# The second layer's filler products on TensorE given up at its three norms

## Chip, cores and metric

The kernel runs on one core of a Trainium2 chip. The metric is the device time in microseconds of one execution; the time before is the median of three.

## Reference

Two transformer blocks one after the other, float32, on 256 tokens of width 1024. The first block and the first layer of the second block (a state-space and attention mixer) are untouched but for the last thing that TensorE does in the mixer. What matters here is the end of that layer and the whole of the last one:

```python
x = x + g1 * mix                                     # end of the hybrid mixer (layer 0)
h = rms_norm(x, norm_ffn_g[0]) * (1 + sc2) + sh2     # norm A
x = x + g2 * swiglu(h, w_gate[0], w_up[0], w_down[0])
h = rms_norm(x, norm_mix_g[1]) * (1 + sc1) + sh1     # layer 1
u = a * sigmoid(gt)            # a, gt = split(h @ w1 + b1)
u = causal_depthwise_conv(u, w_dw, b_dw)             # 31 taps
u = silu(layer_norm(u, ln_g, ln_b))                  # norm B
x = x + g1 * (u @ w2 + b2)
h = rms_norm(x, norm_ffn_g[1]) * (1 + sc2) + sh2     # norm C
x = x + g2 * swiglu(h, w_gate[1], w_up[1], w_down[1])
return rms_norm(x, final_norm_g)
```

`swiglu(h, wg, wu, wd)` is `(silu(h @ wg) * (h @ wu)) @ wd`, hidden width 2816. The document calls the three norms at which the change acts A, B and C.

## The kernel before

Each engine has its own program, written out by hand; semaphores order them. The program is made of blocks (`with nc.Block()`), and at the end of a block all engines meet before any goes on. The mixer of layer 0 is one block, whose end is recorded under line 1790; all that follows, norm A included, is the next.

**Tiling.** The tokens are two halves of 128 (`TT` = 2); the width is 8 pieces of 128 (`KT` = 8). A product of float32 operands is two instructions on TensorE, a transpose is one. Weights stream through a ring of 1 MB slots, filled by SyncE's queue and given back by TensorE (`used`).

**The fillers.** `keep_clock(pe, bank, n)` (line 141) issues n products of the identity with itself, 128x256 out, into a PSUM bank that is free at that place. Nothing waits for them and nobody reads their output. It is called in six places; three of them are touched.

**Norm A.** The mixer's output products (line 2027, `out_half`) end in four parts; VectorE combines each into `X` (lines 2225 and 2227), ScalarE sums the squares (2152). TensorE's last entry in the block is a wait for VectorE's reads (`read_a`) and `keep_clock(pe, 3, 6)`. In the next block VectorE adds up the sums (3138, 3037), ScalarE takes the root (2949), VectorE inverts it and scales the two halves of `X` into `xn` (3046). TensorE turns each half with eight transposes (2698, `turn`), VectorE and ScalarE move the turned pieces with scale and shift into `HT` (3052, 2954), and `first_rows` (2711) starts the first gate product piece by piece as `HT` appears. Then the chunks of the feed-forward part: `half_rows` (2718), the seven-product scheme `seven` (`product`, 2747; `down_part`, 2724; `turn_hid`, 2757), `last_down` (2733).

**Layer 1 up to norm B.** One more norm, with other products of TensorE in its gap (2852, 2858), then the pointwise product, the convolution (part on TensorE, 2873, part on VectorE), the means (2862), `gate_rows` (2858), and the variance (2922). Then `keep_clock(pe, 5, 6)`. ScalarE takes the root (3009), VectorE inverts it (3225) and multiplies (3228), and ScalarE applies silu in eight pieces (3013). The second pointwise product (2932) takes its first eight products one by one as those pieces appear; it has 64 products in all.

**Norm C.** After the last of them `keep_clock(pe, 7, 5)`. VectorE gates and adds the last quarter (3237, 3241), ScalarE sums squares (3020), then as at A: 3243, 3244, 2949, 3042, 3046, the transposes of `turn(2)`, and `ffn(1, 2)`.

Of the kernel before, what the change touches and what calls it, by code (L numbers as in the profile page):

```python
# [66 lines left out]
def _program(nc, t, out, top):  # L67
# [26 lines left out]
    def clear_retired(pool, old):  # L94
        for _, s in old:
            pool.sem_clear(s)
# [9 lines left out]
    def bc(ap, axis, n):  # L106

        v = ap.unsqueeze(axis)
        shape = list(v.shape)
        shape[axis] = n  # L110
        return v.broadcast_to(shape)
# [29 lines left out]
    def keep_clock(pe, bank, n):  # L141

        for _ in range(n):
            pe.matmul(PS[:, bank, 0:S], ident[:], bc(ident[:], 1, 2), start=True, stop=True)
# [153 lines left out]
    with ExitStack() as scope:  # L298
# [60 lines left out]
        def stage_a(k):  # L359
# [19 lines left out]
        FINISH = [("g", 0, 31), ("g", 1, 40), ("r", 0, 48), ("g", 2, 51), ("r", 1, 54), ("g", 3, 57), ("r", 2, 60),  # L379
                  ("g", 4, 67)]  # L380
        square_at = {at: f for f, (_, _, at) in enumerate(FINISH)}
        mean_at = {at + 1: f for f, (_, _, at) in enumerate(FINISH)}
        scale_at = {at + 2: f for f, (_, _, at) in enumerate(FINISH)}
        finish_of = {(kind, j): f for f, (kind, j, _) in enumerate(FINISH)}
# [1226 lines left out]
    with ExitStack() as scope:  # L1611
# [178 lines left out]
        with nc.Block() as block:  # L1790
# [16 lines left out]
            def _(pe):  # L1807
# [237 lines left out]
                pe.wait_ge(read_b, 1)  # L2045
                out_half(1, 1)
                pe.wait_ge(read_a, 2)
                keep_clock(pe, 3, 6)

            @block.scalar  # L2050
            def _(act):
# [602 lines left out]
    with nc.Block() as block:  # L2654
# [38 lines left out]
        def _(pe):  # L2693
            def turn(n):
                for i in range(TT):
                    pe.wait_ge(scaled, TT * n + i + 1)
                    for k in range(KT):
                        mm = pe.transpose(turned_bank(k)[:, i * P:(i + 1) * P],  # L2698
                                          xn[:, i, :].rearrange("p (m k) -> p k m", k=KT)[:, k, :], ident[:])
                        if i == TT - 1:  # L2700
                            mm.then_inc(turned, 1)
# [219 lines left out]
                for m in range(2 * quarter, 2 * quarter + 2):  # L2921
                    mm = pe.matmul(PS[:, 7, 0:S], meanw[:], SQ[:, m, :], start=(m == 0), stop=(m == KT - 1))  # L2922
            mm.then_inc(made, 1)
            keep_clock(pe, 5, 6)
            for c in range(4):
                arrive(pe, B_PW2 + c)
                w = w_slot(B_PW2 + c)
# [4 lines left out]
                        mm = pe.matmul(PS[:, 2 + c, i * CW:(i + 1) * CW], SQ[:, k, i * P:(i + 1) * P], w[:, k, :],  # L2932
                                       start=(k == 0), stop=(k == KT - 1))
                mm.then_inc(used, 1)
            keep_clock(pe, 7, 5)
            turn(2)
            ffn(1, 2)

# [437 lines left out]
```

## Time and profile before

| | |
|---|---|
| time, median of 3 runs | 1472.97 us (1471.86, 1472.97, 1478.15) |
| time of the profiled execution | 1474.04 us |
| its span | 1472.3 us |
| mean granted TensorE clock | 0.981 of full |
| busy: PE, DVE, ACT, POOL | 1382.5, 811.6, 248.1, 259.0 us |

The span runs from the first to the last instruction of the profiled execution, and positions such as "at 903" are microseconds from its start; 1.74 us of that execution's time lie outside its span. PE is TensorE's product instructions, PEld its weight loads, DVE VectorE, ACT ScalarE, POOL GpSimd. The granted clock is given as a share of full speed (2.4 GHz); its other level is half of that.

### The profile page before, as it was taken

The page shows a single profiled execution, that of the slowest core. Times are in us where ns is not written, and L with a number is a line of the kernel's source. Part 1 is how long each engine was busy: PE and PEld are TensorE (multiplying, and loading weights), DVE is VectorE, ACT ScalarE, POOL GpSimd, SP SyncE. Part 2 cuts the span into 40 slices and gives each one's busy share as a digit, 9 for nine tenths or more (in the row PEclk, how much of TensorE's full clock was granted, in tenths as well). Part 3 has the DMA queues.
Part 4 walks back from the last instruction along what each step waited for, and adds up shares of the span by engine and source line. Part 5 has one row for each costly group of instructions (what it writes and reads, how often), then busy time and mean ns, then how long its engine had stood idle before and what let it go on. Part 6 is the DMA issues. An engine that isn't in the chain of part 4 may idle for free. (4 is left out here: it accounts for less than half of the span.)

```text
span 1472.3 us, 18919 instructions
## 1 busy us (share of the span) xinstructions
PE 1382.5 (94%) x7561; PEld 1018.4 (69%) x7561; DVE 811.6 (55%) x1405; ACT 248.1 (17%) x530; POOL 259.0 (18%) x342
## 2 busy tenths in 40 slices
PE   5999999988757999999999999999999999999997
PEld 1877655644333888778888888777776868777774
DVE  2458785332223677853544674888744963544432
ACT  2221211000001211322435101000002032000001
POOL 5078010000001100543436304000021000000000
PEclk9999999998888999999999999999999999999999
DMA  9976788899999588846773456988853633545530
GB/s 345 324 253 230 273 341 328 366 415 416 417 418 369 184 299 290 298 142 157 182 174 117 143 171 201 333 323 326 311 183 103 215 94 115 168 151 168 166 120 29
DMA packets 176055, 355.57 MB, mean 242 GB/s; under 512 B 7289, under 2 KB 137040, under 8 KB 158560
## 3 DMA queue, kind: packets, MB, share of 16 engines
q1 hardware_dynamic: 166720, 313.64, 59.8%
q0 software_dynamic: 9248, 40.71, 9.5%
q8 instruction: 61, 1.00, 0.3%
q14 instruction: 26, 0.21, 0.0%
HBM read 352.58 MB, written 1.74 MB: 241 GB/s over the span
## 5 line engine op out<-in xcount | busy, mean ns | idle before, releaser
L1823 PE MATMUL PS<-HT,ring 128*128 128x256 f32 x1152 | 258.3, 382 | 0.1
L1823 PEld LDWEIGHTS PS<-HT,ring 128*128 128x128 f32 x1152 | 215.5, 190 | 36.0 <-issue 7.9
L2724 PE MATMUL PS<-ring,hid 128*128 128x512 f32 x320 | 143.5, 592 | 0.0
L2724 PEld LDWEIGHTS PS<-ring,hid 128*128 128x128 f32 x320 | 60.8, 190 | 60.3 <-issue 58.4
L2718 PE MATMUL PS<-HT,ring 128*128 128x256 f32 x464 | 101.6, 379 | 0.0
L2718 PEld LDWEIGHTS PS<-HT,ring 128*128 128x128 f32 x464 | 87.8, 190 | 11.8
L1264 PE MATMUL PS<-ring_extra,slot_rows 128*32 128x256 f32 x576 | 54.6, 431 | 27.7 <-DMA ring_extra<-in_expert_w_gate 7.9
L1541 DVE TENSOR_TENSOR X<-X,PS 128x1024 f32<-128x1024 f32 x14 | 17.1, 1221 | 111.6 <-PE PS L1317 111.6
L2747 PE MATMUL PS<-ring,half_sums 128*128 128x256 f32 x288 | 68.1, 379 | 0.0
L2747 PE MATMUL PS<-ada_stage,half_sums 128*128 128x256 f32 x288 | 68.1, 379 | 0.0
L2747 PE MATMUL PS<-ring,HT 128*128 128x256 f32 x288 | 65.2, 379 | 0.0
L2747 PEld LDWEIGHTS PS<-ring,half_sums 128*128 128x128 f32 x288 | 53.5, 190 | 14.3 <-issue 8.6
L1264 PEld LDWEIGHTS PS<-ring_extra,slot_rows 128*32 128x32 f32 x576 | 28.0, 123 | 50.9 <-issue 43.4
L648 PE MATMUL PS<-HT,ring 128*128 128x256 f32 x256 | 60.2, 386 | 0.0
L2747 PEld LDWEIGHTS PS<-ring,HT 128*128 128x128 f32 x288 | 54.6, 190 | 7.4
L2747 PEld LDWEIGHTS PS<-ada_stage,half_sums 128*128 128x128 f32 x288 | 53.5, 190 | 6.6
L3060 DVE SCALAR_TENSOR_TENSOR ada_acc<-ada_stage,ada_c,ada_acc 128x2048 f32<-128x2048 f32 x24 | 56.3, 2346 | 0.3
L648 PEld LDWEIGHTS PS<-HT,ring 128*128 128x128 f32 x256 | 47.9, 191 | 8.5 <-issue 1.4
L2417 DVE SCALAR_TENSOR_TENSOR x_scores<-PS,cums_bias 128x384 f32<-128x384 f32 (+1 forms) x32 | 22.7, 752 | 54.8 <-PE PS L1902 50.5
L2504 POOL TENSOR_TENSOR ssm_weights<-decays,cb_masked 128x384 f32<-128x384 f32 x32 | 35.5, 1126 | 91.0 <-ACT decays L2117 70.4
L2323 DVE SCALAR_TENSOR_TENSOR rows_q<-ada_stage,ada_c,rows_q 128x2048 f32<-128x2048 f32 x14 | 32.9, 2352 | 27.0 <-DMA ada_stage<-in_ada_w 27.0
L645 PE MATMUL PS<-ring,HT 128*128 128x256 f32 x192 | 46.8, 389 | 0.0
(653 smaller groups left out, 2283.4 us busy)
## 6 DMA issues: line engine op xcount, KB each, us to landing
ring<-in_hy_w_in SPq DMA_DIRECT2D x40, 1024.0 KB, 7.5
ring_extra<-in_w_ada SPq DMA_DIRECT2D x24, 1024.0 KB, 8.5
ada_stage<-in_ada_w POOLq DMA_DIRECT2D x24, 1024.0 KB, 7.6
ring<-in_ffn_w_gate SPq DMA_DIRECT2D x22, 1024.0 KB, 5.7
ring<-in_ffn_w_up SPq DMA_DIRECT2D x22, 1024.0 KB, 5.9
ring<-in_ffn_w_down SPq DMA_DIRECT2D x22, 1024.0 KB, 5.1
ring_extra<-in_expert_w_down SPq DMA_DIRECT2D x18, 1024.0 KB, 22.9
ring_extra<-in_expert_w_up SPq DMA_DIRECT2D x18, 1024.0 KB, 20.1
```

Source lines behind the costliest of these rows:

```text
L645: mm = pe.matmul(dst, HT[:, k, half * P:(half + 1) * P], w[:, k, :], start=(k == 0), stop=(k == KT - 1))
L648: mm = pe.matmul(dst, w[:, k, half * P:(half + 1) * P], HT[:, k, :], start=(k == 0), stop=(k == KT - 1))
L1264: mm = pe.matmul(PS[e * SLOTS:(e + 1) * SLOTS, 2, j * CW:(j + 1) * CW], hs[:, k, e * SLOTS:(e + 1) * SLOTS], w[e][:, k, :], start=(k == 0) ...
L1541: dve.tensor_tensor(part, part, PS[:, 6:8, :], ALU.add).then_inc(added, 1)
L1823: mm = pe.matmul(dst, w[:, k, half * P:(half + 1) * P], HT[:, k, :], start=(k == 0), stop=(k == KT - 1))
L2323: dve.scalar_tensor_tensor(out=acc[:, j, :], in0=stage[:], scalar=cv[:, k:k + 1], in1=acc[:, j, :], op0=ALU.mult, op1=ALU.add).then_inc(su ...
L2417: dve.scalar_tensor_tensor(out=SC[:, u % 4, :, 0:n], in0=ps[:, 0:ATT_G, 0:n], scalar=HD ** -0.5, in1=BT[:, 2 * (m % 2) + hd, :, S - n:], o ...
L2504: pool.tensor_tensor(W[:, h % 4, :], dd[:, h % 3, :], cbm[:, h // GH, :], ALU.mult)\
L2718: mm = pe.matmul(dst, w[:, k, m * P:(m + 1) * P], HT[:, k, :], start=(k == 0), stop=(k == KT - 1))
L2724: mm = pe.matmul(PS[:, 4 + 2 * i + h, :], hid[:, par, f, i * P:(i + 1) * P], w[:, f, h * 512:(h + 1) * 512], start=first and f == 0, stop= ...
L2747: mm = pe.matmul(dst, lhs[k], rhs[k], start=(k == 0), stop=(k == KT // 2 - 1))
L3060: dve.scalar_tensor_tensor(out=acc[:, j % 3, :], in0=stage[:, j % 3, :], scalar=cv[:, 2 * i + j // 3:2 * i + j // 3 + 1], in1=acc[:, j % 3 ...
```

## The change

The three calls of `keep_clock` at norms A, B and C are removed: 6, 6 and 5 products, 34 instructions with their weight loads paired to them. Waits, the banks of real results, the order of everything else and the data are as they were. The other three calls (lines 629, 1231 and 1949) stay.

```diff
@@ -2045,7 +2045,6 @@
                 pe.wait_ge(read_b, 1)
                 out_half(1, 1)
                 pe.wait_ge(read_a, 2)
-                keep_clock(pe, 3, 6)
@@ -2921,7 +2920,6 @@
                 for m in range(2 * quarter, 2 * quarter + 2):
                     mm = pe.matmul(PS[:, 7, 0:S], meanw[:], SQ[:, m, :], start=(m == 0), stop=(m == KT - 1))
             mm.then_inc(made, 1)
-            keep_clock(pe, 5, 6)
             for c in range(4):
                 arrive(pe, B_PW2 + c)
@@ -2932,7 +2930,6 @@
                         mm = pe.matmul(PS[:, 2 + c, i * CW:(i + 1) * CW], SQ[:, k, i * P:(i + 1) * P], w[:, k, :],
                                        start=(k == 0), stop=(k == KT - 1))
                 mm.then_inc(used, 1)
-            keep_clock(pe, 7, 5)
             turn(2)
             ffn(1, 2)
```

## Rows read from the trace of the kernel before

**Rows 1.** The page: busy time of TensorE's products; granted clock in 40 slices.

```profile
PE 1382.5 (94%) x7561; PEld 1018.4 (69%) x7561; DVE 811.6 (55%) x1405; ACT 248.1 (17%) x530; POOL 259.0 (18%) x342
...
PEclk9999999998888999999999999999999999999999
```

**Rows 2.** The chain that ended last, in order of time: start, length, what.

```profile
903.45 2.06 PE PS L2698 x16
```

**Rows 3.** Stretches: start:end, length, busy us of PE, PEld, DVE, ACT, POOL, granted clock, DMA.

```profile
903.45:910.45 7.00, 6.94 (x39) 6.03 (x40) 5.46 (x10) 3.22 (x5) 7.00 (x13) 1.00 0.38 90
909.00:1115.00 206.00, 206.00 (x817) 150.76 (x815) 142.98 (x167) 17.08 (x41) 29.00 (x33) 1.00 0.79 286
...
1251.00:1456.00 205.00, 205.00 (x812) 150.21 (x811) 86.86 (x139) 16.99 (x40) 0.00 (x0) 1.00 0.42 139
```

**Rows 4.** Timeline at norm A: start, length, engine, line, [idle before <- what ended it].

```profile
897.03 1.89 PE L2027 MATMUL PS<-x_scores,y_T 128*128 128x256 f32 x8
...
898.75 2.75 PE L144 MATMUL PS<-ident 128*128 128x256 f32 x12
...
900.83 0.19 ACT L2152 ACTIVATION_READ_ACCUMULATOR HT<-X 128x1 f32 x1
901.81 0.16 DVE L3138 TENSOR_REDUCE stat<-stat 128x2 f32<-128x8 f32 x1 [1.34 <-PEq L1790]
...
903.45 2.06 PE L2698 MATMUL PS<-ident,xn 128*128 128x128 f32 x16 [1.95 <-DVE xn L3046]
```

**Rows 5.** Timeline at norms B and C.

```profile
1205.66 3.62 PE L2922 MATMUL PS<-ada_stage,mean_weights 128*128 128x256 f32 x16
...
1212.06 4.04 ACT L3013 ACTIVATE ada_stage<-ada_stage,vec_T 128x256 f32<-128x256 f32 x8 [0.76 <-DVE ada_stage L3228]
...
1212.81 28.22 PE L2932 MATMUL PS<-ring,ada_stage 128*128 128x256 f32 x128 [0.94 <-ACT ada_stage L3013]
...
1240.87 2.32 PE L144 MATMUL PS<-ident 128*128 128x256 f32 x10
...
1245.10 2.05 PE L2698 MATMUL PS<-ident,xn 128*128 128x128 f32 x16 [1.91 <-DVE xn L3046]
```

**Rows 6.** TensorE's timeline where it starts again after an idle stretch elsewhere.

```profile
34.90 1.09 PE L614 MATMUL PS<-ident,merged_T 128*128 128x128 f32 x4 [3.48 <-DVE merged_T L956]
...
246.44 2.02 PE L1215 MATMUL PS<-ident,X 128*128 128x128 f32 x16 [1.78 <-PEq L460]
...
260.56 2.69 PE L1243 MATMUL PS<-pick,normed 128*128 128x128 f32 x11 [1.70 <-DVE pick L1502]
...
390.13 0.64 PE L1264 MATMUL PS<-ring_more,slot_rows 128*32 128x256 f32 x2 [2.94 <-DMA ring<-in_expert_w_up]
...
473.10 5.42 PE L144 MATMUL PS<-ident 128*128 128x256 f32 x24 [2.51 <-PEq L1192]
```

**Rows 7.** Stretches of 7 us from a start after idle time; the clock is the last but two.

```profile
350.10:357.10 7.00, 7.00 (x66) 3.63 (x67) 0.00 (x0) 0.00 (x0) 0.00 (x0) 0.59 1.02 425
...
441.93:448.93 7.00, 6.85 (x68) 3.34 (x68) 0.11 (x1) 0.00 (x0) 0.00 (x0) 0.81 1.02 418
...
473.10:480.10 7.00, 5.74 (x27) 4.77 (x27) 6.59 (x13) 3.73 (x7) 6.57 (x12) 1.00 0.96 288
...
260.56:267.56 7.00, 5.54 (x38) 5.26 (x42) 3.33 (x12) 0.00 (x0) 0.00 (x0) 0.78 1.03 419
```

**Rows 8.** TensorE's timeline, early part: fillers and transposes at either clock.

```profile
35.78 1.92 PE L144 MATMUL PS<-ident 128*128 128x256 f32 x4
37.49 10.97 PE L648 MATMUL PS<-HT,ring 128*128 128x256 f32 x48
...
133.70 0.66 PE L731 MATMUL PS<-ident,ring_extra 128*128 128x128 f32 x4 [1.10 <-DVEq L1012]
```

**Rows 9.** VectorE's timeline: reading PSUM beside the fillers, and with TensorE idle.

```profile
1241.07 0.69 DVE L3237 TENSOR_TENSOR gated<-PS,gate_a 128x512 f32<-128x512 f32 x1 [5.49 <-PE PS L2932]
...
1463.40 0.69 DVE L3133 TENSOR_TENSOR gated<-PS,gate_b 128x512 f32<-128x512 f32 x1 [0.30 <-PE PS L2733]
```

## Prediction

> **What bounds the kernel now.** I read the page first. TensorE's products are busy 94% of the span, and the granted clock is full in all slices but four between 330 and 480 [rows 1]. The chain that ended last shows where TensorE's pace is the kernel's pace. From norm A on it is on TensorE nearly all the way: it leaves the engine at the norms and comes back to it, at A with the transposes at 903.45 [rows 2]; at B and C what it comes back to are line 2932 at 1212.81 and the transposes at 1245.10 [rows 5]. The stretches between them say the same: 206.00 us busy out of 206.00 in the first feed-forward part, 205.00 out of 205.00 in the second, at clock 1.00 [rows 3]. So a microsecond lost by TensorE just after a norm has nothing behind it that takes it back: no transfer and no other engine is waited for there.
>
> The timelines at the norms show the three gaps. At A the last real product ends at 897.03 + 1.89 = 898.92 and the first transpose starts at 903.45 [rows 4]. At B it is 1205.66 + 3.62 = 1209.28 to 1212.81, and at C 1212.81 + 28.22 = 1241.03 to 1245.10 [rows 5]. The fillers stand in these gaps, and after each of them TensorE is idle until VectorE or ScalarE releases it: 1.95, 0.94 and 1.91 us.
>
> **The fillers themselves.** 12 instructions with 2.75 us of busy time at A [rows 4], as many at B, and 10 with 2.32 at C [rows 5]; 7.82 us in all. At B and C they end before the data for the next real product is there, so their own time is hidden under the norm's arithmetic, and taking them out saves nothing there. At A it is different. The fillers are the last thing in their block, and the next block's first instruction on VectorE, at 901.81, was held 1.34 us by TensorE's sequencer at the block's end [rows 4]. The fillers end at 898.75 + 2.75 = 901.50. Without them the last to arrive is ScalarE, whose last instruction ends at 900.83 + 0.19 = 901.02. The block's end opens 901.50 − 901.02 = 0.48 us earlier. **Term 1: −0.48 us.** Its bounds are 0 (if the meeting of engines has a cost of its own after ScalarE) and −0.5.
>
> Do the fillers slow VectorE or ScalarE through a shared port? The gating of a 128x512 piece out of PSUM took 0.69 us beside the fillers, and 0.69 with TensorE idle [rows 9]. Nothing to be had there.
>
> **What the fillers hold off.** Without them the gaps are 898.92 to 902.97 (shorter by term 1), so 4.05 us; 3.53 us; and 4.07 us, all idle. What this kernel's clock does after such idleness can be read elsewhere in the trace. Between its first product and norm A TensorE is idle for 2.9 us or more eight times: 3.48, 4.38, 4.36, 6.09, 2.94, 6.97, 6.10 and 3.15 us, of which the first and the shortest stand in [rows 6]. In all eight the clock granted for the next 7 us is below full: 0.76, 0.61, 0.59, 0.79, 0.77, 0.61, 0.81 and 0.79, of which the lowest and the highest stand in [rows 7]. The longest idle stretch without a fall is 2.51 us, with clock 1.00 after it; of the shorter ones some fell, so the one of 1.70 us at 260.56, with 0.78 after it [rows 6, 7]. The three new gaps lie among the eight, and the gaps left now (1.95, 0.94, 1.91) lie below, with clock 1.00 after norm A [rows 3]. I take it that the clock falls to 1.2 GHz at all three.
>
> **What a fall costs.** With two levels, 1 and 0.5, a mean of c over 7 us means 14 × (1 − c) us at the low level. The eight give 3.36, 5.46, 5.74, 2.94, 3.22, 5.46, 2.66 and 2.94 us, mean 3.97. Work that only the clock limits does half as much in that time, so it loses 1.99 us on average, between 1.33 and 2.87.
>
> Is the work after the norms limited by the clock alone? Plain products are: the four fillers at 35.78 take 37.49 − 35.78 = 1.71 us to the next product, 0.43 each, while twelve in 2.75 us at full clock are about 0.22 each [rows 4, 8]. Transposes nearly: four took 1.09 us at the low clock and 0.66 at full [rows 6, 8], 0.11 more each, so 1.72 for the sixteen after a norm. At A and C they come first, fill most of the low stretch, and the rest goes to `first_rows`, which waits on them; I put the loss at 1.9 rather than 1.99. At B the first products are held back by ScalarE's silu, eight pieces in 4.04 us, 0.5 each [rows 5]. At the low clock a piece's product is two instructions of 0.43, so 0.86: each loses 0.36 instead of 0.43, and 3.97 us hold 4.6 of them, 1.7 us. B's gap is also the shortest, so I count it at 0.9 of that: 1.5.
>
> **Terms 2 to 4: A +1.9, B +1.5, C +1.9.** Bounds: each 0 (no fall) to 2.87.
>
> The sum is −0.5 + 1.9 + 1.5 + 1.9 = +4.8 us. Against the profiled execution's own 1474.04 this is 1478.8. The median of the runs shown is 1.07 us lower, 1472.97, so the predicted time is **1477.8 us**, 0.33% more. The ring's transfers start later by the same microseconds behind TensorE's `used`; with TensorE never waiting over 205 us [rows 3] they have room.
>
> **Where the Trainium skill says otherwise.** After A and C the first work is transposes. That transposes hold the clock in this kernel is shown by the trace: at norm A 1.95 us of idle time are followed by 2.06 us of nothing but transposes, 4.0 us in all and so longer than the shortest idle stretch with a fall (2.94), and the clock stays 1.00 [rows 3, 4]; it did so too after 1.78 us and sixteen transposes at 246.44 [rows 6]. The Trainium skill, "TensorE: Matmul & The Clock Gate", Part 4 (PE-mode transpose), says that the full clock "doesn't engage for transpose-mode", as a transpose does not count as busy in the same way. By that rule the low stretch would not end during the transposes; the result is the second rival. The trace does not agree with it where the clock is full already; that it holds for getting back from the low level, no row of this case excludes.
>
> **The rivals.**
>
> *The clock does not fall, or its fall is hidden* (not slower). For it: B's 3.53 us is not far above the 2.51 that stayed full, and an execution of before may itself fall at A or C now and then, since 1.95 and 1.91 us are more than the 1.70 that fell once [rows 4 to 6]; then the difference shrinks. Against it: 8 of 8. If only one of three falls, −0.5 + 1.9 = +1.4, 1474.4; if none, 1472.5. Chance 0.12.
>
> *The transposes do not bring the clock back* (slower by over 0.5%). Place: norms A and C. The sixteen transposes then run wholly at the low level (+1.72), and the low stretch of 3.97 us is counted from their end, on plain products, +1.99: 3.7 per norm. The sum is −0.5 + 3.7 + 1.5 + 3.7 = +8.4, 1481.4, 0.57% more. It decides if the first gate products (line 2711, now 16 in 3.69 us) run to their end at the low level. For it: the rule above. Against it: [rows 3, 4, 6]. Chance 0.13.
>
> *The fillers held more than the block's end* (faster). It would need 7.4 us, and all three gaps together are 4.53 + 3.53 + 4.07 = 12.1 us, bounded by VectorE's and ScalarE's own chains. Chance 0.02.
>
> **How the numbers follow.** A change of 0.5% (7.4 us) is about what a measurement of this kernel can tell from none; its three runs spread over 6.3 us. The forecast, three falls of ordinary length, has 0.73. Its own range: three short falls −0.5 + 3 × 1.33 = +3.5, three long ones −0.5 + 3 × 2.87 = +8.1; falls of mixed length are likelier, +3 to +6.5. The range of 8 in 10 leaves the case of no fall out at the lower end and takes in the transposes' rival at the upper: 1474.4 to 1481.5. Slower by over 0.5%: 0.12 of the second rival and 0.04 of the forecast's tail, 0.16. Faster by over 0.5%: 0.02. Within 0.5%: 0.82.
>
> **What would show it.** Idle stretches before the transposes at A near 4.05, before line 2932 near 3.53 and before the transposes at C near 4.07 us. At A VectorE's first reduction 0.5 us earlier after the last product, its hold no longer by TensorE's sequencer. Granted clock in the 7 us after each restart at 0.6 to 0.8. Sixteen transposes in 3 to 4 us instead of 2.06. TensorE's own page line down by 34 instructions, but its busy time down by less than 7.8 us. Between the norms everything as long as before. The prediction is wrong if the clock stays 1.00 after two of the gaps, or if the low stretches last much over 5.7 us, or if the feed-forward parts change their length beyond the low stretch.

## The result, and the profile after

Eight runs of each kernel: 1483.21 us after (1479.51 to 1484.89), 1475.74 us before (1471.86 to 1478.15; the first three of these eight are the runs shown above). The ratio is 1.0046, with a 95% interval of 1.0032 to 1.0061: slower by 0.46%, 6.8 us (the two medians themselves lie 7.5 us apart). A second set of twelve runs (e11 below) gave 1.0039, interval 1.0025 to 1.0054. The predicted 1477.8 us and its range up to 1481.5 were too low.

The page's own lines, after:

```profile
span 1481.4 us, 18852 instructions
...
PE 1385.1 (94%) x7527; PEld 1020.0 (69%) x7527; DVE 819.6 (55%) x1405; ACT 248.2 (17%) x530; POOL 263.2 (18%) x342
...
PEclk9999999998989999999999999999999998999999
```

TensorE has its 34 instructions less, as against [rows 1], and is busy 2.6 us longer. VectorE has the same 1405 instructions and is busy 8.0 us longer, which nothing in the prediction foresaw.

Norm A, timeline, after (start, length, engine, line, idle before):

```profile
897.43 1.89 PE L2027 MATMUL PS<-x_scores,y_T 128*128 128x256 f32 x8
...
901.23 0.19 ACT L2151 ACTIVATION_READ_ACCUMULATOR HT<-X 128x1 f32 x1
901.72 0.16 DVE L3135 TENSOR_REDUCE stat<-stat 128x2 f32<-128x8 f32 x1 [0.84 <-PEq L1790]
...
903.36 3.68 PE L2697 MATMUL PS<-ident,xn 128*128 128x128 f32 x16 [4.04 <-DVE xn L3043]
...
906.83 4.74 PE L2710 MATMUL PS<-HT,ring 128*128 128x256 f32 x16
```

Beside [rows 4]: VectorE's hold at the block's end is 0.84 us instead of 1.34, the gap 4.04 instead of 4.53, and the sixteen transposes take 3.68 us instead of 2.06. The 0.84 us are still put down to TensorE's sequencer, which the prediction did not expect. Norms B and C:

```profile
1217.16 0.76 PE L2930 MATMUL PS<-ring,ada_stage 128*128 128x256 f32 x1 [3.54 <-ACT ada_stage L3010]
...
1252.04 3.68 PE L2697 MATMUL PS<-ident,xn 128*128 128x128 f32 x16 [4.07 <-DVE xn L3043]
```

And the clock (third number from the end) over the 7 us behind each restart, which was 1.00 at A in [rows 3]:

```profile
903.36:910.36 7.00, 7.00 (x28) 6.38 (x29) 4.11 (x8) 3.22 (x5) 7.00 (x13) 0.59 0.43 96
1217.16:1224.16 7.00, 7.00 (x19) 5.70 (x20) 2.71 (x6) 4.79 (x9) 0.00 (x0) 0.57 0.00 0
1252.04:1259.04 7.00, 7.00 (x29) 6.42 (x30) 4.11 (x8) 3.42 (x6) 0.00 (x0) 0.63 0.11 36
```

All three fall, and by 14 × (1 − c) they are at the low level for 5.7, 6.0 and 5.2 us of work: three long ones. The rest of the loss is further on, in the first feed-forward part:

```profile
1069.34 2.35 DVE L3057 SCALAR_TENSOR_TENSOR ada_acc<-ada_stage,ada_c,ada_acc 128x2048 f32<-128x2048 f32 x1
...
1072.12 0.42 DVE L3112 TENSOR_TENSOR up_pre<-PS,up_pre 128x256 f32<-128x256 f32 x1 [0.43 <-PE PS L2746]
...
1072.58 0.42 DVE L3114 TENSOR_TENSOR up_pre<-PS,up_pre 128x256 f32<-128x256 f32 x1
1072.64 0.53 POOL L3292 DMA_DIRECT2D ada_stage<-in_ada_w  x1 [15.61 <-DVE ada_acc L3057]
...
1072.92 9.97 DVE L3057 SCALAR_TENSOR_TENSOR ada_acc<-ada_stage,ada_c,ada_acc 128x2048 f32<-128x2048 f32 x1
1073.19 7.54 POOL L3300 TENSOR_TENSOR tap_blocks<-one_block,tap_cols 128x1024 f32<-128x1024 f32 x4
...
1084.25 0.44 PE L2756 MATMUL PS<-ident,hid_rows 128*128 128x128 f32 x2 [1.83 <-DVE hid_rows L3120]
```

VectorE adds the products of the modulation (`ada_acc`) in 24 accumulates of 2.34 us in between its other work. The 22nd takes 9.97 us here, for as long as GpSimd's four multiplications that build `tap_blocks` for the later convolution (7.54 us) and then its own time. TensorE waits 1.83 us for what VectorE does next. In the kernel before the same instructions met otherwise:

```profile
1069.35 2.35 DVE L3060 SCALAR_TENSOR_TENSOR ada_acc<-ada_stage,ada_c,ada_acc 128x2048 f32<-128x2048 f32 x1
...
1071.62 0.42 DVE L3115 TENSOR_TENSOR up_pre<-PS,up_pre 128x256 f32<-128x256 f32 x1
...
1072.07 0.42 DVE L3117 TENSOR_TENSOR up_pre<-PS,up_pre 128x256 f32<-128x256 f32 x1
...
1072.41 2.34 DVE L3060 SCALAR_TENSOR_TENSOR ada_acc<-ada_stage,ada_c,ada_acc 128x2048 f32<-128x2048 f32 x1
...
1073.21 9.11 POOL L3303 TENSOR_TENSOR tap_blocks<-one_block,tap_cols 128x1024 f32<-128x1024 f32 x4
```

There the accumulate is undisturbed and GpSimd is the one held (9.11 us instead of 7.54), where nobody waits for it. What differs ahead of the meeting is the distance between the starts of the 21st and the 22nd accumulate: 3.58 us after, where VectorE waited 0.43 us for TensorE in between (line 3112), and 3.06 us before. GpSimd starts its multiplications 1.50 us after the end of the 21st in both.

**Where the difference of the two profiled executions lies.** Each length is from one of TensorE's starts or ends to another. "A to next" is from A's first transpose to TensorE's last product before the next norm's gap; "pw2" is line 2932's products; "C to end" runs to the last product.

| us | before | after | difference |
|---|---|---|---|
| up to A's last product | 898.92 | 899.33 | +0.41 |
| gap A | 4.53 | 4.03 | −0.50 |
| A to next | 223.52 | 227.97 | +4.45 |
| next norm's gap, up to B | 82.30 | 82.29 | 0 |
| gap B | 3.53 | 3.54 | 0 |
| pw2 | 28.22 | 30.80 | +2.58 |
| gap C | 4.07 | 4.07 | 0 |
| C to end | 218.27 | 220.42 | +2.15 |
| sum, with the tail (8.93 in both) | 1472.3 | 1481.4 | +9.1 |

The first line is not of the change: over all twenty profiles of this study A's last product ended between 896.8 and 903.7. That spread, ahead of everything that the change touches, is as large as that of the timed runs (6.3 us before, 5.4 after). It is why the later lines are read from profiles: for the same falls and the same meeting they repeat within 0.1 us.

### The profile page after: what moved, and what is told of

Read it like the earlier page. It is cut to its first block and busy times, and to the rows that moved or that the text cites. A ratio compares the mean times of both kernels' runs of the same rounds, so it can differ in the third digit from the quotient of the medians.

```text
span 1481.4 us, 18852 instructions
## 1 busy us (share of the span) xinstructions
PE 1385.1 (94%) x7527; PEld 1020.0 (69%) x7527; DVE 819.6 (55%) x1405; ACT 248.2 (17%) x530; POOL 263.2 (18%) x342
## 5 line engine op out<-in xcount | busy, mean ns | idle before, releaser
L3057 DVE SCALAR_TENSOR_TENSOR ada_acc<-ada_stage,ada_c,ada_acc 128x2048 f32<-128x2048 f32 x24 | 63.9, 2664 | 0.3
```

Of the source, the lines that this page charges most:

```text
L3057: dve.scalar_tensor_tensor(out=acc[:, j % 3, :], in0=stage[:, j % 3, :], scalar=cv[:, 2 * i + j // 3:2 * i + j // 3 + 1], in1=acc[:, j % 3 ...
```

## Experiments

There were eighteen runs, e1 to e18; e11 and e12 are the changed kernel and the one before again, e13 and e14 are e9 again, e15 is e1 and e16 is e7 again. e1 to e12 had eight to twelve timed runs each against 31 to 35 of the kernel before; e13 to e18 are one profiled execution each. The lengths in the table are of one profile per row.

| | time, ratio to before (95%) | gap A | A to next | pw2 | C to end |
|---|---|---|---|---|---|
| before | | 4.54 | 223.52 | 28.22 | 218.27 |
| after | 1.0046 (1.0032 to 1.0061) | 4.03 | 227.97 | 30.80 | 220.42 |
| e1 none at A | 1.0034 (1.0019 to 1.0049) | 4.04 | 227.99 | 28.22 | 219.63 |
| e2 none at B | 1.0021 (1.0008 to 1.0035) | 4.53 | 224.88 | 29.61 | 218.27 |
| e3 none at C | 1.0018 (1.0004 to 1.0033) | 4.54 | 223.51 | 28.22 | 220.43 |
| e4 after, taps later | 1.0019 (1.0008 to 1.0031) | 4.04 | 225.97 | 29.61 | 220.36 |
| e5 before, taps later | 0.9996 (0.9984 to 1.0009) | 4.53 | 223.51 | 28.22 | 218.27 |
| e6 transposes as filler | 1.0012 (0.9999 to 1.0026) | 4.35 | 226.87 | 28.22 | 219.55 |
| e7 more filler | 1.0001 (0.9988 to 1.0014) | 4.04 | 223.51 | 28.22 | 218.27 |
| e8 half the filler | 1.0012 (1.0000 to 1.0024) | 4.04 | 223.51 | 29.55 | 219.61 |
| e9 late at A | 1.0024 (1.0012 to 1.0036) | 4.53 | 225.82 | 28.22 | 218.27 |
| e10 late at A, taps later | 1.0014 (0.9998 to 1.0030) | 4.54 | 225.81 | 28.22 | 218.27 |
| e11 after again | 1.0039 (1.0025 to 1.0054) | 4.04 | 227.98 | 30.84 | 220.43 |
| e12 before again | 0.9991 (0.9977 to 1.0006) | 4.54 | 223.51 | 28.22 | 218.27 |
| e13, e14 as e9 | single | 4.54 | 225.81 both | 28.22 | 219.62, 218.27 |
| e15 as e1 | single | 4.04 | 226.69 | 28.22 | 218.27 |
| e16 as e7 | single | 4.04 | 223.51 | 28.22 | 218.27 |
| e17 accumulate 0.5 us later | single | 4.54 | 223.52 | 28.22 | 218.27 |
| e18 accumulate 1 us later | single | 4.54 | 224.86 | 28.22 | 218.27 |

e12 against before shows what two sets of runs of one kernel can differ by: 0.09%, with an interval of −0.23 to +0.06%.

**e1, e2, e3: one norm each.** The edit is one line of the change's diff; e2 and e3 the same at B and C.

```diff
                 pe.wait_ge(read_a, 2)
-                keep_clock(pe, 3, 6)
```

> Only the fillers at norm A are taken out; those at B and C stay. Theory 1 (each gap pays its own fall of the clock, nothing else): the idle stretch before the transposes at A is 4.0 us, the low stretch after it costs 2.0 to 2.9 us, the block's end gives 0.5 back, B and C as in before; +1.5 to +2.4 us in all. Theory 2 (TensorE's lateness at A also brings VectorE's accumulate at about 1073 under GpSimd's four tap multiplications, as in the profile of the changed kernel, 9.97 us instead of 2.34): the same and another 2.1 us between A and the next norm, +3.6 to +4.5 us, with an idle stretch of TensorE near 1082.

> Only the fillers at norm B are taken out. Theory 1: idle stretch 3.53 us, then the clock falls for 3.4 or 6.8 us; line 2932's 64 products take 1.7 to 2.6 us longer than 28.2; nothing else moves. +1.7 to +2.6 us. Rival: the gap of 3.5 us is short enough for the clock to stay in this execution, then 0.

> Only the fillers at norm C are taken out. Theory 1: idle stretch 4.07 us, low stretch after the restart 2.7 to 5.7 us, +1.5 to +2.7 us between the first transpose and the end, nothing else moves. If the three single removals sum to the whole change without the collision at 1073, that collision is a term of its own.

Each removal alone made the kernel slower, and A's the most. The three ratios add up to 0.73%, more than the 0.46% of all three together, but their intervals are too wide to read a sum from them. At A the stage grew by 4.47 us with the 9.94 us accumulate in it: theory 2. The single profiles also show what the shown one of before does not: the clock can fall with the fillers in place. In e2 it fell at A, where nothing was changed, and in e1 at C. Clock over 7 us behind those restarts, e1 at C and then e2 at A and at B:

```profile
1251.15:1258.15 7.00, 7.00 (x32) 6.34 (x33) 4.90 (x9) 3.41 (x6) 0.00 (x0) 0.76 0.13 43
```

```profile
901.35:908.35 7.00, 7.00 (x32) 6.23 (x33) 5.22 (x9) 3.21 (x5) 7.00 (x13) 0.76 0.34 91
1212.06:1219.06 7.00, 7.00 (x24) 5.58 (x25) 2.71 (x6) 4.79 (x9) 0.00 (x0) 0.76 0.00 0
```

These are short falls, 14 × 0.24 = 3.4 us of work at the low level, and cost 1.36 us each (224.88 − 223.52; 219.63 − 218.27), 1.39 at B, where 1.7 to 2.6 had been expected. The fall at A in e2 came without the long accumulate.

**e4 and e5: GpSimd's multiplications moved**, in the changed kernel and in the one before.

```diff
             pool.wait_ge(small, SMALLS)
+            pool.wait_ge(ada_summed, ADDS)
             for at, m in enumerate(PE_TILES):
```

> The changed kernel with GpSimd's four tap multiplications held back until VectorE's 24 accumulates of the modulation are all done. Theory 2 (collision): VectorE's accumulate at about 1073 takes 2.34 us again, TensorE's idle stretch near 1082 is gone, and the part from norm A to the next norm is 2.1 us shorter than in the changed kernel: the loss against before falls from 6.8 to about 4.7 us. Rival (TensorE's lateness itself makes VectorE late): the idle stretch near 1082 stays.

> The control to the run before: the kernel before, fillers in place, with GpSimd's four tap multiplications held back in the same way. In the profile of before the accumulate of VectorE at 1072.41 took 2.34 us beside them, so theory 2 (the collision comes only with a TensorE that is late by more than 1.85 us) expects no change between norm A and the next norm, 223.5 us, and a time within 0.1% of before. Rival (holding the multiplications back is a gain of its own): 1 us or more faster, and then the gain of the run before says nothing on the collision.

In e4 the 22nd accumulate comes as in the changed kernel, 3.59 us after the 21st and behind an addition that waited for TensorE, and is short again:

```profile
1070.77 2.35 DVE L3057 SCALAR_TENSOR_TENSOR ada_acc<-ada_stage,ada_c,ada_acc 128x2048 f32<-128x2048 f32 x1
...
1073.56 0.42 DVE L3112 TENSOR_TENSOR up_pre<-PS,up_pre 128x256 f32<-128x256 f32 x1 [0.43 <-PE PS L2746]
1074.02 0.42 DVE L3114 TENSOR_TENSOR up_pre<-PS,up_pre 128x256 f32<-128x256 f32 x1
1074.36 2.34 DVE L3057 SCALAR_TENSOR_TENSOR ada_acc<-ada_stage,ada_c,ada_acc 128x2048 f32<-128x2048 f32 x1
```

The stage is 225.97 us, 2.00 less than in the changed kernel, with the same long fall at A. The times agree in direction only: the interval of e4's ratio lies below that of the first set of the change and overlaps that of the second (e11, 1.0025 to 1.0054). Part of e4's lower time is also a short fall at B and 0.3 us less behind TensorE's last product, which e5 has too. Between A and the next norm e5's edit gives nothing (223.51 us), and its ratio is 0.9996. So the 2.0 us are the meeting of the two engines, and 2.45 is what the long fall at A costs.

**e6: transposes as filler.**

```diff
-                keep_clock(pe, 3, 6)
+                keep_turned(pe, 3, 22)   # n times pe.transpose(PS[:, bank, 0:P], ident[:], ident[:])
```

and 22 at B, 18 at C.

> Fillers of the same length at A, B and C, but transposes of the identity (22, 22 and 18, some 0.12 us each, 2.6, 2.6 and 2.1 us) instead of products. If transposes hold the clock as products do, no long fall at the three norms, no collision at 1073, and the time of before (within 2 us). If they do not count, the three gaps are idle for the clock for 4.5, 3.5 and 4.1 us and it falls at all three: the time of the changed kernel, about +7 us, with TensorE's idle stretches as short as before.

Neither side came out pure: no fall at B, short falls at A and C, and the long accumulate at 1072.62 (9.94 us). One row bears on the second rival. At C the clock came back to full with nothing but the sixteen transposes behind the fall; the stretch of the transposes, and the one that follows:

```profile
1249.14:1252.61 3.47, 3.47 (x16) 3.47 (x17) 1.64 (x4) 0.18 (x1) 0.00 (x0) 0.51 0.23 80
1252.61:1256.08 3.47, 3.47 (x18) 3.06 (x18) 2.42 (x5) 3.23 (x6) 0.00 (x0) 1.00 0.01 2
```

The rule quoted in the prediction (the Trainium skill, "TensorE: Matmul & The Clock Gate", Part 4) does not hold here. Whether transposes hold the clock as well as products do, one profile cannot say; the idle stretches beside them were also 0.2 us longer at B and C (1.13 and 2.11 us) than in the kernel before.

**e7 and e8: more filler and half of it.** e7 has 4 products before the block's end and 3 behind it at A, 7 at B and 8 at C; e8 has 3, 3 and 2 at the old places.

```diff
-                keep_clock(pe, 3, 6)
+                keep_clock(pe, 3, 4)
@@
+            keep_clock(pe, 3, 3)
             turn(0)
```

> The other way: more filler. A has four products before the block's end and three behind it, B seven instead of six, C eight instead of five. Term 1 of the prediction (the fillers at A hold the block's end by 0.48 us) expects the gap at A to shrink from 4.53 to 4.05 us. Theory 1 expects no fall at the norms in any execution; the kernel before still had short ones of 3.4 us, one at A and one at C in two of the profiles so far, about 1.4 us each. In all 0.5 to 1.5 us less than before.

> Half of the fillers, at the same places: three, three and two products, 1.3, 1.3 and 0.9 us. The idle stretches left are about 3.2 (A, counted with the block's end 0.5 us earlier, 2.8), 2.2 and 3.2 us. Theory 1 with a fall that depends on the idle time left: falls at A and C, mostly short, perhaps none at B; +1.5 to +4 us. Rival (any filler in the gap is enough): the time of before.

e7's gap at A is 4.04 us and no clock fell, as expected, here and in e16; but the time did not move (1.0001, interval 0.9988 to 1.0014), so the 0.5 to 1.5 us are not shown as time. In e8 the idle time left at A was 2.74 us and the clock stayed; at B 2.24 and at C 3.21 us, and it fell for a short time at both, the reverse at A and B of what had been expected:

```profile
903.68:910.68 7.00, 6.94 (x39) 6.03 (x40) 5.47 (x10) 3.21 (x5) 7.00 (x13) 1.00 0.42 98
1213.04:1220.04 7.00, 7.00 (x25) 5.87 (x26) 2.70 (x6) 4.78 (x9) 0.00 (x0) 0.76 0.00 0
1246.66:1253.66 7.00, 7.00 (x33) 6.45 (x34) 4.58 (x8) 3.42 (x6) 0.00 (x0) 0.76 0.13 41
```

The longer idle stretch stayed full and the shorter one fell: in one execution the length of the idle stretch alone does not decide. That any filler in the gap is enough is not borne out either: at B the clock never fell with six products, and fell here with three.

**e9, e10, e13, e14: TensorE late at full clock.** Six more products behind A's transposes; e10 has e4's edit too.

```diff
             turn(0)
+            keep_clock(pe, 3, 6)
             ffn(0, 0, turn_vectors, modulation_rows)
```

> The kernel before, with six more filler products (2.6 us at full clock) put behind the transposes of norm A: TensorE is late into the feed-forward part as in the changed kernel, but the clock stays full. If lateness alone sends VectorE's accumulate under GpSimd's multiplications, the accumulate near 1072 takes about 9.9 us, and the part from the first transpose of A to the next norm grows from 223.5 by 2.6 and another 2.0 us, to 228.1. If the collision needs the low clock, it grows by 2.6 only, to 226.1.

> The same with GpSimd's four tap multiplications held back until VectorE's 24 accumulates are done. If the 2.0 us are the meeting of the two engines, the part from A to the next norm is 226.1 us; if they are lateness of VectorE by itself, 228.1 again.

> As e9, another execution. If lateness of TensorE is enough: where the ninth weight sum starts less than 159.6 us after norm A's first transpose, VectorE's accumulate is released by TensorE, starts 0.27 us ahead of GpSimd's multiplications and takes 9.9 us, and the part from A to the next norm is 227.8 us; where it starts later, 2.34 us and 225.8. If the low clock is needed: 225.8 in either case.

> The same kernel once more, and the same expectation: 227.8 us from A to the next norm where the ninth weight sum starts less than 159.6 us after norm A's first transpose, 225.8 where it starts later.

The long accumulate did not come in e9, e13 or e14. VectorE's waits (total us, times, longest) show why in e9: its ninth sum of weights was held by a transfer. The kernel before has the same wait, a little shorter; the changed kernel has none on a transfer there, and waits for TensorE twice at line 3112. From e9, before and after:

```profile
DVE ada_stage L3079 <- DMA ring<-in_ffn_w_up: 2.6, 1, 2.6
...
DVE ada_stage L3078 <- DMA ring<-in_ffn_w_up: 2.2, 1, 2.2
...
DVE up_pre L3112 <- PE PS L2746: 0.9, 2, 0.4
```

In e9 VectorE was then the late one, not TensorE, and the 22nd accumulate started 3.06 us after the 21st and 0.8 us ahead of GpSimd, as in before:

```profile
1076.47 2.35 DVE L3061 SCALAR_TENSOR_TENSOR ada_acc<-ada_stage,ada_c,ada_acc 128x2048 f32<-128x2048 f32 x1
...
1079.53 2.34 DVE L3061 SCALAR_TENSOR_TENSOR ada_acc<-ada_stage,ada_c,ada_acc 128x2048 f32<-128x2048 f32 x1
1079.78 0.53 POOL L3296 DMA_DIRECT2D ada_stage<-in_ada_w  x1 [18.31 <-DVE ada_acc L3061]
...
1080.33 7.23 POOL L3304 TENSOR_TENSOR tap_blocks<-one_block,tap_cols 128x1024 f32<-128x1024 f32 x3
```

In e13 and e14 the ninth sum started 159.2 us after A's first transpose, under the 159.6 for which I had expected the collision, and there was none: the bound was wrong. What counts is whether the transfer is the one waited for: it held the sum by 0.40 and 0.44 us in e13 and e14, and not at all in e10, where the sum started at 158.7. Over all profiles with GpSimd's multiplications in their old place (but e17 and e18, below) the spacing of the two accumulates parts them cleanly. It was 3.58 us, TensorE being waited for, in after, e1, e6, e11 and e15, and the accumulate took 9.9 us in all five; it was 3.1 in before, e2, e3, e7, e8, e9, e12, e13, e14 and e16, and it took 2.34 in all ten. The transfer parts the same two groups: it held the ninth sum in all ten, by 0.40 to 2.60 us, and in none of the five. And since GpSimd's start followed the end of the 21st accumulate by 1.50 us in all of them, the spacing fixes the lead over GpSimd, 0.27 us in the five and 0.8 in the ten. So neither a late TensorE nor a fall of the clock is enough to bring the spacing of 3.58 us: e2 and e15 both had a short fall at A; in e2 the transfer held the sum by 1.56 us and the accumulate took 2.34 us, in e15 it did not and the accumulate took 9.94. e10 had the 3.58 at full clock, but there GpSimd's part was moved. So lateness of TensorE at full clock brings the accumulate into the same place; that it brings the collision is not shown.

**e17 and e18: only the accumulate late.**

```diff
+                if n == 21:
+                    dve.memset(tmp[:, 0, :], 0.0)      # e18: tmp[:]
                 dve.scalar_tensor_tensor(out=acc[:, j % 3, :], in0=stage[:, j % 3, :],
```

> The kernel before with one memset of 512 elements on VectorE (about 0.3 to 0.6 us) ahead of its 22nd accumulate, the one near 1072; its data are used by nobody. If the order of arrival decides, the accumulate starts 0.2 to 0.5 us ahead of GpSimd's multiplications and takes 9.9 us; VectorE is then free some 179 us after norm A's first transpose and the part from there to the next norm is 227.4 to 228 us, 4 us more than before, though no clock fell. If the low clock is needed, the accumulate takes 2.3 us and the part stays at 223.5.

> The same with a memset of 1024 elements (0.6 to 1.1 us), so that the accumulate starts about with GpSimd's multiplications or behind them. If the order of arrival decides: as in the run before, 9 to 10 us for the accumulate, 227 to 228.5 us from A to the next norm. If a lead of less than 0.8 us is not what decides: 2.3 us and 223.5.

```profile
1077.02 0.48 DVE L3061 MEMSET gated<- 128x512 f32 x1
1077.13 0.53 POOL L3297 DMA_DIRECT2D ada_stage<-in_ada_w  x1 [17.64 <-DVE ada_acc L3062]
...
1077.42 2.23 DVE L3062 SCALAR_TENSOR_TENSOR ada_acc<-ada_stage,ada_c,ada_acc 128x2048 f32<-128x2048 f32 x1
1077.67 9.52 POOL L3305 TENSOR_TENSOR tap_blocks<-one_block,tap_cols 128x1024 f32<-128x1024 f32 x4
```

In e17 the accumulate started 0.25 us ahead of GpSimd, closer than the 0.27 of the changed kernel, and was not held; GpSimd was. In e18 GpSimd started 0.29 us ahead of it, and again GpSimd was held (10.06 us for its four) while the accumulate took 2.23; the 1.34 us in e18's stage are a short fall at A. The theory that the order of the recorded starts decides has fallen. The memset also changes what runs just ahead of the accumulate, so these two runs do not show that the low clock is needed either.

**e11, e12, e15, e16: kernels run again.**

> The changed kernel a second time, for another profile and more runs. Theory 1: the clock falls at A, B and C again, for 3.4 or 6.8 us each; a fall of 6.8 us costs 2.45 (A), 2.58 (B) or 2.15 us (C), one of 3.4 us costs 1.36 to 1.39. Theory 2: the collision (2.0 us) comes with a long fall at A. Stages before norm A as in before within their own spread of some 4 us. Ratio again 1.003 to 1.006.

> The kernel before as if it were a change: shows what two groups of runs of one kernel differ by (ratio 1.000 within 0.0015), and one more profile of whether the clock falls at A or C in spite of the fillers.

> As e1, another execution. A fall of the clock at A; a long one (6.8 us) costs 2.45 and a short one 1.36 us. With the long one, the ninth weight sum near 158.8 us after the first transpose and the collision, 228.0 us; with a short one the collision only if the transfer is early.

> As e7, another execution: no fall of the clock at A, B or C; gap at A 4.04 us; from A's first transpose to the end of the products as short as in the kernel before, 223.5, 80.8, 28.2 and 218.3 us.

e11 repeats the changed kernel's profile: three long falls and the accumulate of 9.94 us. e15 had a short fall at A, and the accumulate of 9.94 us with it: 226.69 us. A stage with the long accumulate ends about 48.4 us after that accumulate does (1082.89 to 1131.33 in after, 1082.30 to 1130.74 in e15), whatever came first.

**Counts over all profiles.** Without fillers in its gap the clock fell 13 times of 13 (A 5, B 4, C 4), ten times for long (after and e11 at all three, e4 at A and C, e1 at A, e3 at C) and three times shortly (e2 and e4 at B, e15 at A). With the old fillers it fell at A in 2 of 11 profiles, at C in 2 of 12 and at B in 0 of 12, each time shortly. With more filler (e7, e16) it fell in none of six, with half of it or with transposes (e8, e6) shortly in two of three each. Costs read from the stages: long 2.45 us at A, 2.58 to 2.62 at B, 2.09 to 2.16 at C; short 1.34 to 1.36 at A, 1.33 to 1.39 at B, 1.28 to 1.36 at C.

## Why the prediction was wrong

**What held.** TensorE's pace behind the norms is the kernel's pace: every loss there arrived at the end undiminished. Term 1 was right: −0.48 foreseen, −0.50 measured, and the gaps were 4.04, 3.54 and 4.07 us for 4.05, 3.53 and 4.07. All three clocks fell. The direction held. That the change is under 0.5% is not shown either way: the ratio is 1.0046, but its interval reaches 1.0061.

**How the miss adds up.** The forecast was +4.8 us. The two profiled executions differ by 9.1: 0.4 ahead of A, which is not of the change, −0.5 of term 1, 7.2 of the falls and 2.0 of the meeting on VectorE. So two terms failed, the falls by 1.9 us and the missing one by 2.0, and the base under the sum by 2.8. The measured 1483.21 lies 1.7 us above the range; each of the three misses is larger than that by itself.

**The first failed step: "A +1.9, B +1.5, C +1.9".** Each term stayed within its bound of 2.87, but all three were under-sized. The falls measured 2.45, 2.58 and 2.15 us, 7.2 together where the prediction had 5.3. I took the mean of eight falls, 3.97 us at the low level, over idle stretches from 2.9 to 7.0 us. The three new ones had 5.7, 6.0 and 5.2: that is the part mis-sized. The cost per microsecond at the low level was put too high rather than too low: 2.45 of 5.7, 2.58 of 6.0 and 2.15 of 5.2 are 0.43, 0.43 and 0.41, where the sum had 0.48 at A and C and, with silu's pace, 0.43 at B before the discount for its short gap. So the allowance for silu was right, that for the transposes too small, and the further 0.9 at B had no counterpart in the shown profile. A neighbour of like idle time would have helped at A and C, where the two nearest (4.38 and 4.36 us) had 5.46 and 5.74, but not at B, where the nearest (3.48 us) had 3.36. Idle time does not order the eight (6.09 and 6.10 us had 2.94 and 2.66), nor does it decide afterwards: behind the same 3.54 us B's fall was long in two profiles and short in two (e2, e4), and behind 4.04 us A's was short once (e15). A forecast of one execution has two sizes to choose from, long or short, and ten of the thirteen falls were long.

**The second failed step: "Between the norms everything as long as before".** This term was put at nothing without a reason: the prediction did not ask which engines work beside the delayed TensorE 170 us later. Instead "A to next" lost another 2.0 us to VectorE's accumulate and GpSimd's multiplications, shown by e4 against the changed kernel, with e5 as its control. The rivals had no such case. The prediction's own last sign of being wrong, a feed-forward part that changes its length beyond the low stretch, is what came. The trace of before held the hint: 9.11 us for GpSimd's four where 7.5 is their own time, a pair of engines already in each other's way, 0.8 us apart; and VectorE waited there for a transfer, 2.2 us, so that TensorE had some time to be late in before VectorE would wait for it instead. In the range this was not priced.

**The base.** The sum was put on the median of three runs, 1472.97. With eight it is 1475.74, 2.8 us higher, and three later sets gave 1475.46, 1476.58 and 1476.96. On 1475.74 the forecast of +4.8 would have been 1480.5, and the range 1477.2 to 1484.3, with the measured 1483.21 in it. The three runs' own spread of 6.3 us was named and then left out of the range. The profiles put it ahead of norm A for the most part (6.9 us over all twenty), and some of it on short falls at A and C that the kernel before has in some executions. Those falls, and short ones in the changed kernel, would also make the difference of the sets (5.8 and 6.8 us by their ratios) smaller than the 9.1 of the two profiled executions; how much each gives is not shown.

**The rivals.** The clock's staying up did not come at any norm in the changed kernel. The rival of the transposes failed too: the gate products of line 2710 took 4.74 us after A, not the 6.9 that it needs, and in e6 at C the clock came back behind transposes alone. The argument against it was weaker than it read, though. It set 4.0 us of idle time and transposes against 2.94 as the shortest idle stretch with a fall, where [rows 6, 7] have a fall after 1.70; and the fillers and transposes of A did not hold the clock in two of eleven profiles. The granted clock was also not full in all slices but four, as the prediction has it: its own [rows 6, 7] have falls behind the restarts at 34.90 and 260.56, in slices that the page marks 9, which is 90% or more.

**What stays open.** Why VectorE's accumulate and not GpSimd's multiplication is held when the additions ahead of it waited for TensorE. e4 shows that the meeting costs 2.0 us, and fifteen profiles that it goes with the spacing of 3.58 us; e17 and e18 exclude that the recorded starts alone decide. No run has the 3.58 us at full clock with GpSimd in its old place. Open too is which falls are long and which short, and why half the filler let it fall after 2.24 us and not after 2.74.

## What to carry over

Filler products on the engine that sets the pace pay in two ways: they keep the clock (2.1 to 2.6 us for a long fall here, about 1.35 for a short one) and they keep the schedule in step, and a delay of 1.4 to 2.5 us can cost another 2 where two other engines then meet. Price a fall as a short or a long one and not by a mean of both, and look for pairs of engines that already slow each other, downstream of the delay. A filler that stands last in a block holds the other engines at the block's end (0.5 us here); and a sum is worth as much as the base that it is put on: with runs 6 us apart, three are too few for a range of 7 us.

## What the runs showed of the hardware that was not expected

A VectorE accumulate of two SBUF inputs, 2.34 us by itself, was held through four GpSimd multiplications in a row, 9.9 us, though its recorded start was 0.27 us the earlier. The Trainium skill, "SBUF — State Buffer", section "SBUF: two separate sides", says of the port pair that the two engines share that a VectorE instruction with two SBUF inputs and a GpSimd instruction that reads SBUF exclude each other, and that whichever starts first has the pair "for the whole instruction". That one waits for the other whole is what the rows show, and here through four instructions in a row; that the first to start wins, e1, e6, e11, e15 and the changed kernel contradict, going by recorded starts, and e18 from the other side, where GpSimd started first by 0.29 us and was the one held.

The same idle stretch, with the same fillers, is followed by a fall of the clock in some executions and not in others: 1.91 to 1.95 us of idle time at A and C, four falls in 23.
